# Splitting the two late norms of a two-block transformer layer between two output units, with weight halves placed between the tiles, and folding the end of the last product

## Chip, cores and metric

One NeuronCore of a Trainium2 chip runs the whole program. The metric is device time in microseconds (us); the median of several executions is compared.

## Reference

Two blocks run one after the other on x, a 256 x 2048 float32 matrix (sequence x width). The change touches the end of the second block only:

```python
        mix = (gate_a * ya + gate_b * yb) @ w_out[i]
        h = h + rmsnorm(mix, g_mix_post[i])
        u = rmsnorm(h, g_ffn_pre[i])
        up = causal_depthwise_conv_2(u @ w_up[i], conv_w[i], conv_b[i])
        gate_ff, value = jnp.split(up, [D_FF_2], axis=-1)
        f = (jax.nn.gelu(gate_ff, approximate=True) * value) @ w_down[i]
        h = h + rmsnorm(f, g_ffn_post[i])
        e = p[i] @ w_ple_in[i]
        h = h + jax.nn.sigmoid((h @ w_ple_gate[i]).astype(jnp.float32)).astype(h.dtype) * e
```

## The kernel before

Activations lie transposed: width on the 128 partitions (16 tiles of 128), the 256 positions along the free axis. Every product is made of **units**: a unit is 256 output columns over the whole inner dimension, and one unit is four **pieces** of four k tiles each (three pieces in ffn_down2). A piece's weights are one 512 KB transfer into `raw`. ScalarE casts them to their high half (`w_high`), VectorE subtracts to get the low half (`w_low`), and TensorE forms high x high, high x low and low x high, so the sum is nearly exact float32. Rings of four slots hold raw, high and low, so a piece's high half can be cast only when TensorE has finished the piece four before it.

A unit accumulates in one of two PSUM banks, `ps`, which alternate. Left half of a bank: products with x's high half; right half: high weights with x's low half. When the unit is done ScalarE copies the right half (`bcopy`), VectorE adds it (`summ`), and the unit's epilogue follows. In a **folded** unit both products go to the left half, in six matmuls of 256 columns for a k tile instead of two of 512 and two of 256; such a unit needs no copy and no add.

`Phase` objects list the products; `unit_no`, `piece_no`, `after` give the semaphore values. Each engine runs its own program in written order, and waits on semaphores for the others. `skewed` and `threaded` interleave the weight halves of later units with the epilogue of a unit.

The two **late norms** are the places where x has to be made new from the sum of squares of a whole product:

- **First late norm**, after `w_out2_end`: h + rmsnorm(mix), then the gain of the next norm; x goes into `act_a`, and `ffn_up0` (u @ w_up) reads it. The division by the second norm's rms is deferred to that product's epilogues (`rms(4)`, `recip(4)`, then `summ * rstd`). Its sum of squares is the matmul group `ssq_h`, which before stands after half of ffn_up0's second unit.
- **Second late norm**, after `ffn_down2_end`: h + rmsnorm(f); x goes into `act_a` for `ple_gate`.

In both, TensorE runs `gap`: the sum of squares, with the product p @ w_ple_in (8 groups of six matmuls, "ple") as filler around it. ScalarE takes the root (`rms`), VectorE the reciprocal (`recip`). `post_norm` then makes the tiles two at a time: VectorE scales (L1826), VectorE or GpSimd adds to the residual (L1831, L2048: pairs 0, 3, 6 on VectorE, the other five on GpSimd), ScalarE makes x's high half (L1356 or L1359), VectorE its low half (L1838 or L1843). The first unit of the next product takes the tiles as they come (`need_pn`), the weights of its four pieces having been prepared ahead of the norm.

The program ends with `ple_gate`, 8 units: sigmoid(h @ w) times e (in `gates`), added to h by GpSimd (L1963) and stored.

Of the kernel before, what the change touches and what calls it, by code (L numbers as in the profile page):

```python
# [21 lines left out]
ALU = mybir.AluOpType  # L22
# [100 lines left out]
def last_direct(ph, j):  # L123

    return ph.name in ("w_out2_end", "ffn_down2_end") and j == ph.U - 1


def plan():
# [23 lines left out]
    for g, n in enumerate((8, 8, 6)):  # L152
        ph.append(Phase("upconv", 2 * n, 2, 4, name=f"ffn_up{g}", group=g))
# [6 lines left out]
    ph.append(Phase("final", 8, 2, 4, name="ple_gate"))  # L160
# [58 lines left out]
def build(nc, A, out):  # L219
# [4 lines left out]
    with ExitStack() as ctx:  # L224
# [48 lines left out]
        def pcol(name, i=0):  # L273
# [67 lines left out]
        def source(ph, i, j, s):  # L341
# [26 lines left out]
            elif n.startswith("ffn_up"):  # L368
                w, c = "w_up_2", i * 256 + (j * DFF2 + ph.group * D)
# [6 lines left out]
            else:  # L376
                w, c = "w_ple_gate_2", u * 256
# [3 lines left out]
        def slot(ph, j, s):  # L381
            return (2 * s + j if ph.name == "proj_0" else j * ph.ppu + s) % RING
# [112 lines left out]
        def dst_tile(ph, i, j):  # L495
# [18 lines left out]
            if ph.kind == "upconv":  # L514
                return i * 2
# [12 lines left out]
        ADD_DVE, ADD_POOL = (0, 3, 6), (1, 2, 4, 5, 7)  # L528
# [42 lines left out]
        def _(sp):  # L571
# [24 lines left out]
            for ph in PH[1:]:  # L596
                def body(i, ph=ph):
                    for j in range(ph.U):
                        for s in range(ph.ppu):
                            n, at = piece_no(ph, i, j, s), slot(ph, j, s)  # L600
                            src = source(ph, i, j, s)
                            kn = src.shape[1]
                            sp.wait_ge(split_done, n + 1)
                            sp.dma_start(raw[:, at, 0:kn * S].rearrange("p (t n) -> p t n", t=kn),
                                         src).then_inc(raw_full[at], 16)
                over(sp, body, 0, ph.bodies)

            fin = BY["ple_gate"]
# [7 lines left out]
        def _(pe):  # L616
# [84 lines left out]
            for s in range(4):  # L701
                for j in range(2):
                    piece(p0, from_buf(act_a), None, 0, j, s, need_x)
# [35 lines left out]
            def gap(n, ph, ple_ph):  # L739
# [3 lines left out]
                take(fill, 1)  # L743
                ssq_last(ph)
                take(fill)

# [224 lines left out]
            gap(3, BY["w_out2_end"], BY["ple0"])  # L971
# [6 lines left out]
            def ssq_h():  # L978

                pe.wait_ge(pn_added, 2)  # L980
                pe.wait_ge(rms_ready, 4)
                parts = [sqacc[:, 0, :], sqacc[:, 1, :], G[:, 24, :], G[:, 25, :]]
                for c, part in enumerate(parts):
                    last = nc.tensor.matmul(pm[:, 3, 0:S], ones, part, start=(c == 0), stop=(c == 3))
# [8 lines left out]
            gap(5, BY["ffn_down2_end"], BY["ple1"])  # L993
            units(BY["ple_gate"], from_buf(act_a), None, lambda: None, need_pn(16))
# [3 lines left out]
        def _(act):  # L998
# [23 lines left out]
            def epilogue(ph, i, j):  # L1022
                k, g, n = ph.kind, bank(ph, j), unit_no(ph, i, j)
                t0 = dst_tile(ph, i, j)
                if last_direct(ph, j):
                    if k == "mix":
# [8 lines left out]
                act.wait_ge(w_used, end_piece(ph, i, j))  # L1035
                act.wait_ge(summed, n + 1)
                nc.scalar.copy(bcopy[:, g], ps[:, g, :, S:2 * S]).then_inc(b_copied, 1)  # L1037
# [32 lines left out]
            def stages(ph, i, j):  # L1070
# [14 lines left out]
                def base():  # L1085
# [4 lines left out]
                    c0 = i * 2 + (16 * ph.group + 44 * j)  # L1090
# [250 lines left out]
            def post_norm(n, ph, ple_ph, gain):  # L1341

                half = ple_ph.half
                rms(n)
# [3 lines left out]
                ple_out(ple_ph, 0)  # L1348
                for b in range(8):
                    if b in ADD_DVE:  # L1350
                        act.wait_ge(pn_r_dve, len(ADD_DVE) * half + ADD_DVE.index(b) + 1)
                    else:
                        act.wait_ge(pn_r_pool, len(ADD_POOL) * half + ADD_POOL.index(b) + 1)
                    if gain:
                        for k in (2 * b, 2 * b + 1):
                            nc.scalar.activation(act_a[:, k, 0:S], PJ[:, k, :], ACT.Copy,  # L1356
                                                 scale=pcol(gain, k)).then_inc(pn_high, 1)
                    else:
# [750 lines left out]
```

## Time and profile before

| | |
|---|---|
| median of 3 executions | 2986.57 us (2985.01 to 2989.87) |
| profiled execution: its own time | 2986.37 us |
| profiled execution: span | 2984.6 us |
| TensorE busy | 2939.8 us, 99% of the span |
| VectorE, ScalarE, GpSimd busy | 1915.2, 1533.6, 247.0 us |
| mean granted TensorE clock | 0.997 of full |

TensorE is busy nearly all the time, so the span is its work plus the few places where it waits. Times in the rows are microseconds from the span's start. The first late norm lies at about 2107 to 2145, the second at about 2863 to 2902, and the end is at 2977 to 2984.

### The profile page before, as it was taken

To read this page: it belongs to the slowest core of one execution; us is meant where nothing else is said; L and a number is where in the kernel's file an instruction comes from. 1 tells how busy PE (TensorE), PEld (TensorE's weight loads), DVE (VectorE), ACT (ScalarE), POOL (GpSimd) and SP (SyncE) were. 2 spreads that over 40 slices of the span, in tenths; PEclk is the share of its full clock that TensorE was granted. 3 is DMA by queue.
4 is the path that set the end of the run, shared out by engine and by line. 5 is a ranking of instruction groups with operands and counts; after the bars stand their busy time and mean duration, and the time that the engine had idled before them with its cause. 6 is when DMAs were issued, how large, how long until landed. Compare 5 with 4: busy or idle time off the path is not lost. (4 is left out here: it accounts for less than half of the span.)

```text
span 2984.6 us, 49193 instructions
## 1 busy us (share of the span) xinstructions
PE 2939.8 (99%) x17298; PEld 2583.4 (87%) x17298; DVE 1915.2 (64%) x2171; ACT 1533.6 (51%) x1909; POOL 247.0 (8%) x204
## 2 busy tenths in 40 slices
PE   8999999999999999999999999999999999999999
PEld 7888898988888888888888888988788888888877
DVE  6586665556665656656656666655777567657664
ACT  5576644444544444444544446445566455545554
POOL 3010020102101010000200000001200000010121
PEclk9999999999999999999999999999999999999999
DMA  8565557665566665665665545656466666566545
GB/s 241 162 175 159 169 179 218 190 172 188 189 190 190 190 190 183 197 188 180 197 190 178 169 149 166 197 169 199 147 196 184 190 189 190 185 188 190 169 150 161
DMA packets 543393, 544.85 MB, mean 183 GB/s; under 512 B 17096, under 2 KB 541896, under 8 KB 543280
## 3 DMA queue, kind: packets, MB, share of 16 engines
q1 hardware_dynamic: 541184, 537.32, 58.6%
q0 software_dynamic: 2096, 6.07, 0.7%
q8 instruction: 65, 1.06, 0.2%
q14 instruction: 48, 0.39, 0.0%
HBM read 541.23 MB, written 2.10 MB: 182 GB/s over the span
## 5 line engine op out<-in xcount | busy, mean ns | idle before, releaser
L1399 DVE TENSOR_TENSOR w_low<-raw,w_high 128x1024 fp32r<-128x1024 f32 x1016 | 1254.6, 1250 | 813.7 <-ACT w_high L1012 807.0
L1012 ACT CAST w_high<-raw 128x1024 fp32r<-128x1024 f32 x1016 | 1051.9, 1049 | 979.5 <-PE ps_gemm L649 945.0
L644 PE MATMUL ps_gemm<-act_a,w_high 128*128 128x512 f32 x4480 | 1449.0, 396 | 22.0 <-DVE act_a L1552 9.9
L644 PE MATMUL ps_gemm<-act_b,w_high 128*128 128x512 f32 x3208 | 1046.1, 396 | 6.9 <-DVE act_b L1408 4.6
L649 PEld LDWEIGHTS ps_gemm<-act_a,w_low 128*128 128x128 f32 x4608 | 865.2, 189 | 154.4
L649 PE MATMUL ps_gemm<-act_a,w_low 128*128 128x256 f32 x4608 | 993.7, 279 | 0.0
L644 PEld LDWEIGHTS ps_gemm<-act_a,w_high 128*128 128x128 f32 x4480 | 720.1, 189 | 69.5 <-issue 11.1
L649 PE MATMUL ps_gemm<-act_b,w_low 128*128 128x256 f32 x3520 | 780.0, 279 | 0.0
L649 PEld LDWEIGHTS ps_gemm<-act_b,w_low 128*128 128x128 f32 x3520 | 653.9, 189 | 97.3
L644 PEld LDWEIGHTS ps_gemm<-act_b,w_high 128*128 128x128 f32 x3208 | 524.9, 188 | 50.5 <-issue 4.9
L1441 DVE TENSOR_TENSOR summ<-ps_gemm,bcopy 128x512 f32<-128x512 f32 x227 | 155.4, 685 | 19.2 <-ACT bcopy L1037 19.1
L1037 ACT COPY bcopy<-ps_gemm 128x512 f32<-128x512 f32 x242 | 140.2, 579 | 22.5 <-PE ps_gemm L649 22.4
L1936 POOL TENSOR_TENSOR proj<-proj,summ 128x512 f32 x32 | 41.4, 1292 | 1008.0 <-DVE summ L1441 1008.0
L1510 DVE SCALAR_TENSOR_TENSOR gates<-summ,params,gates 128x254 f32<-128x254 f32 (+1 forms) x176 | 77.3, 481 | 18.6 <-ACT gates L1093 11.2
L1452 DVE TENSOR_TENSOR summ<-summ,rstd 128x512 f32<-128x512 f32 x124 | 85.9, 692 | 4.3
L1922 POOL TENSOR_TENSOR proj<-proj,summ 128x512 f32 x32 | 55.6, 1737 | 374.2 <-DVE summ L1496 374.2
L639 PE MATMUL ps_gemm<-act_b,w_high 128*128 128x256 f32 x312 | 82.6, 286 | 2.5 <-DVE proj L1491 2.3
L641 PE MATMUL ps_gemm<-act_b,w_high 128*128 128x256 f32 x312 | 82.3, 285 | 0.0
L1057 ACT CAST act_a<-summ 128x512 f32 (+1 forms) x32 | 19.9, 622 | 96.8 <-DVE summ L1465 96.8
L639 PEld LDWEIGHTS ps_gemm<-act_b,w_high 128*128 128x128 f32 x312 | 60.5, 194 | 2.9 <-issue 2.9
L1044 ACT ACTIVATE gates<-summ 128x512 f32<-128x512 f32 (+1 forms) x40 | 25.3, 632 | 69.5 <-DVE summ L1452 69.4
L641 PEld LDWEIGHTS ps_gemm<-act_b,w_high 128*128 128x128 f32 x312 | 60.6, 194 | 0.0
(285 smaller groups left out, 1227.1 us busy)
## 6 DMA issues: line engine op xcount, KB each, us to landing
raw<-in_w_in SPq DMA_DIRECT2D x352, 512.0 KB, 4.2
raw<-in_w_up SPq DMA_DIRECT2D x176, 512.0 KB, 3.5
raw<-in_w_mlp_up SPq DMA_DIRECT2D x128, 512.0 KB, 3.9
raw<-in_w_mlp_down SPq DMA_DIRECT2D x128, 512.0 KB, 3.5
raw<-in_w_down SPq DMA_DIRECT2D x88, 512.0 KB, 4.6
raw<-in_w_out SPq DMA_DIRECT2D x64, 512.0 KB, 4.7
raw<-in_w_branch SPq DMA_DIRECT2D x32, 512.0 KB, 4.3
raw<-in_w_ple_gate SPq DMA_DIRECT2D x32, 512.0 KB, 4.5
```

The source lines that it names most:

```text
L639: nc.tensor.matmul(ps[:, g, t, 0:S], wh[:, at, o:o + P], high(x), start=first, stop=False, skip_group_check=True)
L641: nc.tensor.matmul(ps[:, g, t, 0:S], wh[:, at, o:o + P], x[:, S:2 * S], start=False, stop=False, skip_group_check=True)
L644: nc.tensor.matmul(ps[:, g, t, :], wh[:, at, o:o + P], x, start=first, stop=False, skip_group_check=True)
L649: return nc.tensor.matmul(ps[:, g, t, 0:S], wl[:, at, o:o + P], high(x), start=False, stop=final, skip_group_check=True)
L1012: nc.scalar.copy(wh[:, at, :], raw[:, at, :]).then_inc(high_ready, 1)
L1037: nc.scalar.copy(bcopy[:, g], ps[:, g, :, S:2 * S]).then_inc(b_copied, 1)
L1399: nc.vector.tensor_tensor(wl[:, at, :], raw[:, at, :], wh[:, at, :].bitcast(F32), ALU.subtract).then_inc(split_done, 1)
L1441: nc.vector.tensor_tensor(s2, A_half, bcopy[:, g], ALU.add).then_inc(summed, 1)
L1452: nc.vector.tensor_tensor(s2, s2, r2, ALU.mult).then_inc(scaled, 1)
L1510: last = nc.vector.scalar_tensor_tensor(out=y[:, t, sh:S], in0=summ[:, g, t, 0:S - sh], scalar=pcol("conv_w2", c0 + t + 88 * tap), in1=y[: ...
L1922: nc.gpsimd.tensor_tensor(d, d, s2, ALU.add).then_inc(merged if split else epi_done, 1)
L1936: nc.gpsimd.tensor_tensor(d, d, s2, ALU.add).then_inc(epi_done, 1)
```

## The change

Around both late norms the next product's first two units form a phase of their own (`ffn_up0_0`, `ple_gate_0`). They are **woven**: TensorE runs piece s of unit 0 and then piece s of unit 1, so that a quarter of x (four tiles) is used by two units before the next quarter is needed. VectorE now makes every add, and GpSimd has none; the first four tiles go one at a time, the others in pairs. The casts and subtractions of the weight halves stand between the tiles. The sums of squares of the first norm are added by VectorE (`add_squares`), and `ssq_h` stands after the first unit of the remaining `ffn_up0`. Two units' epilogues then follow by hand. The table for the root is loaded ahead of the last square. At the second late norm ScalarE copies the third unit of ffn_down2_end and casts the first high half before it squares. The last two units of ple_gate are a phase `ple_gate_end`, whose second unit is folded: ScalarE takes the sigmoid straight from PSUM and VectorE makes the last add.

The core of the diff:

```diff
 def last_direct(ph, j):
-    return ph.name in ("w_out2_end", "ffn_down2_end") and j == ph.U - 1
+    return ph.name in ("w_out2_end", "ffn_down2_end", "ple_gate_end") and j == ph.U - 1
...
+def steps(ph):
+    if woven(ph):
+        return [(j, s) for s in range(ph.ppu) for j in range(ph.U)]
+    return [(j, s) for j in range(ph.U) for s in range(ph.ppu)]
...
 # TensorE
+            def two_units(ph, buf, need):
+                for j, s in steps(ph):
+                    piece(ph, from_buf(buf), None, 0, j, s, need if j == 0 else None)
...
-                    units(BY["ffn_up0"], from_buf(act_a), None, ssq_h, need_pn(0), (1, 1))
+                    two_units(BY["ffn_up0_0"], act_a, need_pn(0))
+                    units(BY["ffn_up0"], from_buf(act_a), None, ssq_h)
...
 # ScalarE, from the root on
                 rms(n)
+                ple_out(ple_ph, 0)
+                for k in range(4):
+                    high_x(k)
+                ple_out(ple_ph, 1)
                 gain_post(ph.kind, 14)
+                high_x(4, 2)
+                squares(0)
+                piece(then, 0, 0, 2)
+                high_x(6, 2)
+                high_x(8, 2)
+                squares(4)
+                high_x(10, 2)
+                piece(then, 0, 1, 2)
+                piece(then, 0, 0, 3)
...
 # ScalarE, after the first late norm
+            copy_half(w0, 0, 0)
+            piece(w1, 0, 0, 0)
+            copy_half(w0, 0, 1)
+            for s in range(1, 4):
+                piece(w1, 0, 0, s)
+            piece(w1, 0, 1, 0)
+            rms(4)
+            gate, value = stages(w0, 0, 0), stages(w0, 0, 1)
+            gate[1]()
+            piece(w1, 0, 1, 1)
+            value[1]()
+            gate[3]()
+            piece(w1, 0, 1, 2)
+            piece(w1, 0, 1, 3)
+            value[3]()
...
 # ScalarE, after the second late norm
+            epilogue(w0, 0, 0)
+            piece(w1, 0, 0, 0)
+            epilogue(w0, 0, 1)
+            for s in range(1, 4):
+                piece(w1, 0, 0, s)
...
 # VectorE
+            def add_norm(half, k, n=1):
+                dve.wait_ge(pn_gain, 8 * half + k // 2 + 1)
+                nc.vector.tensor_tensor(t, PJ[:, 16 + k:16 + k + n, :], r2, ALU.mult).then_inc(pn_t, n)
+                dve.wait_ge(pn_t, 16 * half + k + n)
+                nc.vector.tensor_tensor(d, d, t, ALU.add).then_inc(pn_r, n)
...
+                if k == "final" and last_direct(ph, j):
+                    dve.wait_ge(acted, after("acted", ph, i, j))
+                    nc.vector.tensor_tensor(s2, s2, tiles(G, t0, 2), ALU.mult).then_inc(scaled, 1)
+                    nc.vector.tensor_tensor(tiles(PJ, t0, 2), tiles(PJ, t0, 2), s2, ALU.add).then_inc(epi_done, 1)
```

Three places in the order of the built programs carry the prediction.

VectorE in the first late norm, before: from the reciprocal (gates is the scaled product, proj the residual, act_a is x).

```order
L1538 RECIPROCAL rstd<-rms 128x256 [waits rms_ready]
L1826 TENSOR_TENSOR gates<-proj,rstd 128x512 [waits pn_gain,rstd_ready]
L1831 TENSOR_TENSOR proj<-proj,gates 128x512 [waits pn_t]
L1826 TENSOR_TENSOR gates<-proj,rstd 128x512 [waits pn_gain] x3
L1838 SCALAR_TENSOR_TENSOR act_a<-proj,params,act_a 128x256 [waits pn_high]
L1838 SCALAR_TENSOR_TENSOR act_a<-proj,params,act_a 128x256
L1831 TENSOR_TENSOR proj<-proj,gates 128x512 [waits pn_t]
```

The changed program on VectorE, tiles 4 to 7 of the same norm and what follows them:

```order
L1938 TENSOR_TENSOR gates<-proj,rstd 128x512 [waits pn_gain]
L1940 TENSOR_TENSOR proj<-proj,gates 128x512 [waits pn_t]
L1947 SCALAR_TENSOR_TENSOR act_a<-proj,params,act_a 128x256 [waits pn_high]
L1947 SCALAR_TENSOR_TENSOR act_a<-proj,params,act_a 128x256
L1938 TENSOR_TENSOR gates<-proj,rstd 128x512 [waits pn_gain]
L1940 TENSOR_TENSOR proj<-proj,gates 128x512 [waits pn_t]
L1947 SCALAR_TENSOR_TENSOR act_a<-proj,params,act_a 128x256 [waits pn_high]
L1947 SCALAR_TENSOR_TENSOR act_a<-proj,params,act_a 128x256
L1484 TENSOR_TENSOR w_low<-raw,w_high 128x1024 [waits high_ready]
```

A pair's scale, add and low half now stand right behind each other, where three scales stood in a row before, and weight halves have moved in among the pairs.

ScalarE at the second root of the first late norm, before: the last square, the four high halves of the second unit, then the root.

```order
L1364 ACTIVATE gates<-proj 128x1024
L1012 CAST w_high<-raw 128x1024 [waits w_used,raw_full0]
L1012 CAST w_high<-raw 128x1024 [waits w_used,raw_full1]
L1012 CAST w_high<-raw 128x1024 [waits w_used,raw_full2]
L1012 CAST w_high<-raw 128x1024 [waits w_used,raw_full3]
L1126 ACTIVATE rms<-ps_small,stat 128x256 [waits rstd_ready,ssq_ready]
```

The same place in the changed program; the first cast is that of piece 0 of unit 1 of ffn_up0, the later three those of its pieces 1, 2 and 3.

```order
L1040 CAST w_high<-raw 128x1024 [waits w_used,raw_full0]
L1164 ACTIVATE rms<-ps_small,stat 128x256 [waits rstd_ready,ssq_ready]
L1131 ACTIVATE gates<-summ,params 128x256 [waits scaled,epi_done]
L1131 ACTIVATE gates<-summ,params 128x256
L1040 CAST w_high<-raw 128x1024 [waits w_used,raw_full1]
L1131 ACTIVATE gates<-summ,params 128x256 [waits scaled]
L1131 ACTIVATE gates<-summ,params 128x256
L1139 ACT_TABLE_LOAD [waits epi_done]
L1139 ACTIVATE gates<-gates 128x512 [waits acted]
L1040 CAST w_high<-raw 128x1024 [waits w_used,raw_full2]
L1040 CAST w_high<-raw 128x1024 [waits w_used,raw_full3]
```

Three of the unit's four high halves have moved from ahead of the root to behind it.

ScalarE after the second late norm in the changed program, from the last weight half of `ple_gate_0` on; the casts behind are pieces 0 and 1 of the next unit. Before, eight casts stood here ahead of the first copy.

```order
L1040 CAST w_high<-raw 128x1024 [waits w_used,raw_full3]
L1055 COPY bcopy<-ps_gemm 128x512 [waits summed,w_used]
L1106 ACT_TABLE_LOAD
L1106 ACTIVATE summ<-summ 128x512 [waits summed]
L1040 CAST w_high<-raw 128x1024 [waits w_used,raw_full0]
L1055 COPY bcopy<-ps_gemm 128x512 [waits summed,w_used]
L1106 ACTIVATE summ<-summ 128x512 [waits summed]
L1040 CAST w_high<-raw 128x1024 [waits w_used,raw_full1]
```

A unit's whole epilogue now stands ahead of the next unit's first weights.

## Rows read from the trace of the kernel before

**Rows 1.** The page, busy time, share of the span and instructions.

```profile
PE 2939.8 (99%) x17298; PEld 2583.4 (87%) x17298; DVE 1915.2 (64%) x2171; ACT 1533.6 (51%) x1909; POOL 247.0 (8%) x204
```

**Rows 2.** Waits of TensorE: in total, times, longest (us).

```profile
PE ps_small L715 <- ACT sqt L1111: 1.1, 1, 1.1
```

**Rows 3.** Stretches: length, busy PE, PEld, DVE, ACT, POOL, clock, DMA share, GB/s.

```profile
2095.77:2107.29 11.52, 11.52 (x98) 11.52 (x97) 5.44 (x5) 6.12 (x8) 1.29 (x1) 1.00 0.63 191
2114.91:2118.59 3.68, 0.01 (x2) 0.03 (x1) 3.68 (x4) 2.13 (x5) 3.25 (x2) 0.87 0.01 2
2118.59:2124.39 5.80, 5.77 (x17) 4.63 (x18) 5.80 (x8) 4.39 (x8) 3.77 (x3) 0.50 0.00 0
2124.39:2137.37 12.98, 9.88 (x49) 7.65 (x49) 12.95 (x18) 8.00 (x12) 4.88 (x4) 1.00 0.01 1
...
2804.79:2806.97 2.18, 0.40 (x4) 0.19 (x2) 1.36 (x2) 1.40 (x2) 0.00 (x0) 1.00 0.08 26
2806.97:2810.72 3.75, 3.75 (x12) 3.17 (x13) 3.50 (x3) 2.06 (x3) 0.00 (x0) 0.54 0.26 81
2880.81:2885.25 4.44, 0.00 (x1) 0.03 (x1) 4.44 (x5) 2.70 (x4) 3.31 (x2) 1.00 0.01 4
2885.25:2888.91 3.66, 3.66 (x13) 3.13 (x14) 3.66 (x5) 1.31 (x3) 1.90 (x2) 0.55 0.00 0
2888.91:2899.35 10.44, 9.88 (x53) 8.17 (x53) 9.09 (x11) 6.04 (x7) 3.10 (x2) 0.99 0.01 2
2902.19:2977.55 75.36, 75.35 (x433) 65.56 (x432) 39.40 (x38) 37.27 (x42) 12.37 (x7) 1.00 0.58 184
```

**Rows 4.** VectorE, groups by form: count, busy, mean ns of one, idle before.

```profile
L1399 DVE TENSOR_TENSOR w_low<-raw,w_high 128x1024 fp32r<-128x1024 f32 x1016 | 1254.6, 1250 | 813.7 <-ACT w_high L1012 807.0 <-DVEq L1494 3.1
...
L1452 DVE TENSOR_TENSOR summ<-summ,rstd 128x512 f32<-128x512 f32 x124 | 85.9, 692 | 4.3
...
L1510 DVE SCALAR_TENSOR_TENSOR gates<-summ,params,gates 128x255 f32<-128x255 f32 x88 | 38.7, 481 | 12.9 <-ACT gates L1093 11.2
...
L1826 DVE TENSOR_TENSOR gates<-proj,rstd 128x512 f32<-128x512 f32 x16 | 16.0, 1021 | 0.1
...
L1408 DVE TENSOR_TENSOR act_a<-proj,act_a 128x256 fp32r<-128x256 f32 x20 | 7.5, 419 | 2.6 <-ACT act_a L1299 1.5 <-ACT act_a L1259 1.1
```

**Rows 5.** ScalarE, groups by form, the same columns.

```profile
L1012 ACT CAST w_high<-raw 128x1024 fp32r<-128x1024 f32 x1016 | 1051.9, 1049 | 979.5 <-PE ps_gemm L649 945.0 <-DMA raw<-in_w_in 32.6 <-DMA raw<-in_w_out 0.3
...
L1093 ACT ACTIVATE gates<-summ,params 128x256 f32<-128x256 f32 x88 | 48.2, 596 | 23.2 <-DVE summ L1452 20.6 <-issue 0.4
...
L1356 ACT ACTIVATE act_a<-proj,params 128x256 fp32r<-128x256 f32 x16 | 7.1, 500 | 7.3 <-POOL proj L2048 4.7 <-DVE proj L1831 2.6
```

**Rows 6.** VectorE and ScalarE in order of time: start, length, instruction.

```profile
2110.95 1.75 DVE L1538 RECIPROCAL rstd<-rms 128x256 f32<-128x256 f32 x1 [0.52 <-ACT rms L1126]
...
2152.28 1.28 ACT L1101 ACT_TABLE_LOAD   x1
2153.57 0.63 ACT L1101 ACTIVATE gates<-gates 128x512 f32<-128x512 f32 x1
...
2875.55 1.28 ACT L1126 ACT_TABLE_LOAD   x1
2876.85 0.47 ACT L1126 ACTIVATE rms<-ps_small,stat 128x256 f32<-128x256 f32 x1
...
2877.35 1.75 DVE L1538 RECIPROCAL rstd<-rms 128x256 f32<-128x256 f32 x1 [0.56 <-ACT rms L1126]
```

**Rows 7.** The end, in order of time.

```profile
2977.58 0.59 ACT L1037 COPY bcopy<-ps_gemm 128x512 f32<-128x512 f32 x1 [7.52 <-PE ps_gemm L649]
2978.20 0.69 DVE L1441 TENSOR_TENSOR summ<-ps_gemm,bcopy 128x512 f32<-128x512 f32 x1 [7.41 <-ACT bcopy L1037]
2978.92 0.63 ACT L1068 ACTIVATE summ<-summ 128x512 f32<-128x512 f32 x1 [0.76 <-DVE summ L1441]
...
2980.70 1.26 POOL L1963 TENSOR_TENSOR proj<-proj,summ 128x512 f32 x1 [8.27 <-DVE summ L1472]
```

More of the change, by code:

```diff
@@ L700, in need_x @@
                     pe.wait_ge(lo0, 4 * s + k + 1)
-            for s in range(4):
-                for j in range(2):
-                    piece(p0, from_buf(act_a), None, 0, j, s, need_x)
+            for j, s in steps(p0):
+                piece(p0, from_buf(act_a), None, 0, j, s, need_x)
             def ssq_before(n, ph):
@@ L737, in ple, with gap @@
                         yield
-            def gap(n, ph, ple_ph):
+            def gap(n, ph, ple_ph, ahead):
                 fill = ple(ple_ph)
                 ssq_before(n, ph)
-                take(fill, 1)
+                take(fill, ahead)
                 ssq_last(ph)
                 take(fill)
+            def two_units(ph, buf, need):
+                for j, s in steps(ph):
+                    piece(ph, from_buf(buf), None, 0, j, s, need if j == 0 else None)
             pe.wait_ge(in_common, 16)
@@ L978, in ssq_h @@
             def ssq_h():
-                pe.wait_ge(pn_added, 2)
+                pe.wait_ge(pn_added, 1)
                 pe.wait_ge(rms_ready, 4)
-                parts = [sqacc[:, 0, :], sqacc[:, 1, :], G[:, 24, :], G[:, 25, :]]
-                for c, part in enumerate(parts):
-                    last = nc.tensor.matmul(pm[:, 3, 0:S], ones, part, start=(c == 0), stop=(c == 3))
+                for c in range(4):
+                    last = nc.tensor.matmul(pm[:, 3, 0:S], ones, G[:, 16 + c, :], start=(c == 0), stop=(c == 3))
                 last.then_inc(ssq_ready, 1)
@@ L1034, in epilogue @@
                     return
[L1035 to L1037 removed]
+                if not copied:
+                    copy_half(ph, i, j)
                 if k == "gate":
@@ L1347, in post_norm @@
                 gain_post(ph.kind, 14)
[L1348 to L1358, printed above, removed]
-                        nc.scalar.copy(act_a[:, 2 * b:2 * b + 2, 0:S], PJ[:, 2 * b:2 * b + 2, :]).then_inc(pn_high, 2)
-                    if b == 1:
-                        ple_out(ple_ph, 1)
-                    if gain and b % 2:
-                        t = 2 * b - 2
-                        nc.scalar.activation(G[:, 16 + t:20 + t, :], PJ[:, t:t + 4, :], ACT.Square).then_inc(pn_sq, 1)
-            def first_pieces(ph, pend):
-                for s in range(3):
-                    piece(ph, 0, 0, s)
-                pend()
-                piece(ph, 0, 0, 3)
+                high_x(4, 2)
[7 more added lines that the diff above has]
+                piece(then, 0, 0, 3)
+                high_x(12, 2)
+                squares(8)
+                high_x(14, 2)
+                piece(then, 0, 1, 3)
+                squares(12)
             pend = phases(["w_out2"], pend)
@@ new lines, in post_norm @@
+            def post_norm(n, half, gain, then, fourth):
+                recip(n)
+                add_norm(half, 0)
+                add_norm(half, 1)
+                low_x(half, gain, 0)
+                add_norm(half, 2)
+                low_x(half, gain, 1)
+                add_norm(half, 3)
+                low_x(half, gain, 2)
+                low_x(half, gain, 3)
+                if fourth:
+                    piece(then, 0, 1, 1)
+                add_norm(half, 4, 2)
+                low_x(half, gain, 4, 2)
+                add_norm(half, 6, 2)
+                low_x(half, gain, 6, 2)
+                piece(then, 0, 0, 2)
+                add_norm(half, 8, 2)
+                low_x(half, gain, 8, 2)
+                add_norm(half, 10, 2)
+                low_x(half, gain, 10, 2)
+                piece(then, 0, 1, 2)
+                piece(then, 0, 0, 3)
+                add_norm(half, 12, 2)
+                low_x(half, gain, 12, 2)
+                add_norm(half, 14, 2)
+                low_x(half, gain, 14, 2)
+                piece(then, 0, 1, 3)
@@ L1888, in _ @@
-            post_norm(5, 1, None)
-            dve.wait_ge(epi_done, BY["ple1"].unit0 + 2 + 2)
-            pend = skip_first(BY["ple_gate"])
-            pend()
+            down, w0, w1 = BY["ffn_down2_end"], BY["ple_gate_0"], BY["ple_gate"]
+            pieces(down, 0, 0)
+            pend()
+            for j in range(3):
+                pieces(down, 0, j + 1)
+                epilogue(down, 0, j)
+            piece(w0, 0, 0, 0)
+            piece(w0, 0, 1, 0)
+            epilogue(down, 0, 3)
@@ L2065, in _ @@
             run("ffn_down2_end")
-            for b in ADD_POOL:
-                add(b, 1)
+            run("ple_gate_0")
             run("ple_gate")
+            run("ple_gate_end")
 def kernel(**inputs):
```

273 lines of the change are left out of this document (166 added, 107 removed).

## Prediction

> **What bounds the kernel now.** I read the page first. TensorE is busy 99% of the span [rows 1], so only three things can move the time: TensorE's work, the places where it waits, and what follows its last matmul. The view of its waits and a table of stretches place the idle time at the two late norms; the timeline then gives the order in which each engine works there, the groups by form give durations.
>
> The unit of account is a piece (four k tiles). The undisturbed stretch before the end holds 432 matmuls, 27 pieces of 16, in 75.36 us: 2.79 us a piece, 11.17 a unit. A folded unit takes 11.52 [rows 3].
>
> At the first late norm the filler ends at 2114.91. The first unit then would end at 2126.1, yet unit 1 starts at 2137.37: TensorE stands 3.68 us, runs 5.80 us at a granted clock of 0.50 and is then fed slowly, and 11.3 us are lost. At the second the filler ends at 2880.81, unit 0 at 2899.35 instead of 2892.0: 7.4 us lost, with 4.44 us of standing and 3.66 us at 0.55 [rows 3]. A further 1.1 us are waited for the last square [rows 2]. These 20 us are what there is to win.
>
> **First norm, the tiles.** TensorE's need falls to four tiles in 5.58 us, since two units use each quarter. The question is how fast VectorE makes them. The 16 scales of before take 1.02 us each in the mean, where the same shape takes 0.69 elsewhere [rows 4]; beside them GpSimd was adding. With no GpSimd work there I use 0.69. A wait on an op just finished costs some 0.04 us (the end's chain goes from 2978.92 + 0.63 on in such steps, and 2977.58 + 0.59 to 2978.20) [rows 7]. A following independent op starts about 0.1 before the one ahead ends: 0.60 and 1.14 us of pitch for 0.69 and 1.25, an estimate from the timeline.
>
> In the new order scale, add, high half and low half of a pair are one chain: 0.73 + 0.73, then two 256-wide activations on ScalarE (0.50 each, second 0.39 later, so 0.93 with the wait) [rows 5], then two low halves of 0.48, 0.40 apart: 3.2 us a pair, in which VectorE stands idle while ScalarE casts. Two pairs and two weight halves of 1.14 [rows 4] make 8.7 us for a quarter, not 5.58. So VectorE sets the pace still.
>
> The start: the root's table load now lies ahead of the last square, so the reciprocal comes some 0.4 earlier than 2110.95 [rows 6] and ends at 2112.3. Four single tiles (0.42 an op [rows 4]) take 4.9, to 2117.2. Six pairs take 19.1, three weight halves between them 3.4, waits for their high halves 0.2, the last weight half 1.3: 2141.2. Woven unit 1's last piece ends at 2144.0. Before, unit 1 ended, ssq_h aside, at 2137.37 + 11.17 = 2148.5. **Won: 4.5 us.**
>
> **First norm, the handover.** Here I look at what stands behind the new waits. Ahead of ssq_h only piece 0 of ffn_up0's unit 1 has its halves; pieces 1, 2 and 3 have their casts behind the second root on ScalarE. After ssq_h TensorE has 2.79 us of work. Piece 1 needs: the sum's drain 0.36 (an estimate from the timeline), root 0.47, reciprocal 1.75 [rows 6], scale 0.69 [rows 4], base of the convolution 1.0 (two activations of 0.60, overlapping), cast 1.05 [rows 5], low half 1.25 [rows 4], six hand-overs 0.2: 6.8 us. TensorE stands 4.0 us. Then piece 2: four taps of 0.48 (1.9), scale 0.69 [rows 4], base 1.0, table load 1.28, gelu 0.6 [rows 6], cast 1.05, low half 1.25, less 0.1 of overlap: 7.6 us against 2.9: it stands 4.7. Before, all four pieces were ready here. The first two pieces of ffn_up0 cost 0.3 (low halves behind sums), and each restart 0.1. **Lost: 9.2 us.** The norm together: +4.7 us. The DMAs are not late: piece n's transfer starts when piece n-4 is split, and the stretches in question ran at up to 0.01 of the DMA engines [rows 3].
>
> **Second norm.** Third unit's copy and the first cast are ahead, so the last add doesn't wait behind three weight halves, the 1.1 us of [rows 2] go and the table load (2875.55) is off the path: reciprocal at 2875.6 instead of 2877.35 [rows 6], end 2877.4. No gain here, so high and low half are one op of 0.62 and 0.69: 2.7 us a pair. Four single tiles 4.7, six pairs 16.3, four weight halves 4.6 with waits, the last one 1.3, some 0.4 of waiting for it: 2904.7; unit 1's last piece ends at 2907.5. Before, unit 1 ended at 2899.35 + 11.17 = 2910.5. Won: 3.0. The handover: from the end of unit 0, copy 0.6 [rows 7], sigmoid's table 1.28, sigmoid 0.6, cast 1.05, low half 1.25 make 4.7 against 2.79 (with drain): 2.1 us stall; then product, sum, sigmoid, cast, low half, 4.1 against 2.9: 1.2 us; restarts 0.2. Lost: 3.5. The folded unit adds 11.52 - 11.17 = 0.35. **Together: +0.85 us.**
>
> **The end.** Before: copy, sum, sigmoid, product, then GpSimd to 2981.96 from 2977.58 [rows 7], 4.38 us. Now sigmoid 0.63, product 0.69, add 0.69 with waits 0.07: 2.1. **-2.3 us.** The last transfer is as before.
>
> **TensorE's clock.** A tile takes 0.70 us at 2.4 GHz. After standing for 3.68, 4.44 and most of 2.18 us it ran 5.80, 3.66 and 3.75 us at 0.50 to 0.55, the 1.2 GHz level [rows 3]; 12 or 13 matmuls in 3.7 us instead of 2.1 is 1.6 us lost a time. The change takes away the first two and puts in stalls of 4.0, 4.7 and 2.1 us and several of 1 to 1.8. Inside a norm, or just ahead of another stall, the slow clock costs nothing, since VectorE is awaited; behind the 4.7 and the 2.1 it is exposed, in part. Nothing here shows how much: between 0 and three such stretches (4.8 us) I take one and a half, 2.5 us.
>
> The Trainium skill's page "TensorE: Matmul & The Clock Gate" (HAM oscillation — how this bites in real kernels) says that idle gaps between bursts bring the throttle back, each next burst starting cold, which speaks against an order that trades one long gap for several. By that rule each stall of handover length would pay, and the sum would take the upper bound, +2.3 us; the rows with 0.50 to 0.55 agree for gaps from 2.2 us up.
>
> **The sum**: +4.7 + 0.85 - 2.3 + 2.5 = +5.75 us on the profiled execution's 2986.37: 2992.1. The median of the runs lies 0.2 above that execution, so 2992.2 us, +0.19%.
>
> **Rivals.**
> - *The clock stays full* behind the new stalls. For it: the stalls are split, and waits of 1.1 to 1.3 us brought no slow stretch. Against: 2.18 us did [rows 3]. 2992.2 - 2.5 = 2989.7.
> - *The clock falls at each, or hops cost more.* Three exposed stretches add 2.3; if a hop costs 0.1 instead of 0.04, the 36 hops of the twelve pairs add 2.2, about half of them on the path with the rest of the chain: together 2996.
> - *The handover costs half*, because VectorE and ScalarE get ahead of the order I assumed. Only the written order speaks, and it is against it. 2992.2 - 4.4 - 1.0 (less slow clock) = 2986.8, no change at all.
> - *The other side: VectorE keeps pace.* If a pair took 2.2 us or less, a quarter would cost TensorE's 5.58 and no tile would be awaited: unit 1 would end at 2114.9 + 22.3 = 2137.2 and, with the filler 1.1 earlier, at 2879.7 + 22.3 = 2902.0: 6.8 and 5.5 us sooner, with some slow clock gone: 2979. For it: the slowed scales show how much GpSimd's adds took [rows 4]. Against: the chain's own durations.
> - *A drain at each table load.* The table load costs its 1.28 us again at each switch. In the trace the gelu starts at 2153.57, 0.01 after the load's end [rows 6], so it costs 1.28 and no more. If another 1.4 us went with each of the two loads that are newly on the path, the time would be 2995. The Trainium skill's page "ScalarE: Activation LUTs" (What ACT_TABLE_LOAD costs) puts the whole switch at 2.66 us, 1.38 of them a drain; the trace does not agree.
>
> **How the numbers follow.** What a measurement can tell from no change is about 0.2%, 6.0 us. The forecast has 0.56, its own range 2990.0 to 2994.5, half on each side of 2992.5; full clock 0.13; clock or hops 0.14; half the handover 0.09; pace kept 0.05; drain 0.03. Faster 0.05. Within: 0.28 + 0.13 + 0.09 = 0.50. Slower: 0.28 + 0.14 + 0.03 = 0.45. The range takes in full clock and reaches into the half handover below and the clock's case above: 2987 to 2996.5.
>
> **What the changed profile would show.** TensorE's waits for x (now L664 on L1947, L1951) come in several pieces of 0.2 to 1.8 us in either norm, where single ones of 3.68 and 4.44 stood; none over 2 us. No GpSimd add, and scales of 0.69 us. Two stalls of some 4.0 and 4.7 us on `w_low` within 12 us, 50 us after the first norm's start, and two of 2.1 and 1.2 us behind ple_gate_0. The end: sigmoid, product, add, 2.1 us to the last transfer. Wrong would be: no stall on `w_low` after ssq_h, pairs made in 2.2 us, or a slow stretch in each of the gaps.

## The result and the profile after

| | before | after |
|---|---|---|
| median | 2986.57 us (2983.44 to 2989.87, 9 runs) | 2993.51 us (2992.84 to 3000.91, 9 runs) |
| ratio after / before | | 1.0028, 95% interval 1.0019 to 1.0037 |
| profiled execution, span | 2984.6 us | 2993.5 us |

The change makes the kernel slower. The medians differ by 6.9 us (0.23%); the ratio of 1.0028 is worked out over all runs, and one of after's, 3000.91, stands far from the rest. The forecast was 2992.2 (+0.19%). The profiled execution of after took 2995.9 us, 2.4 above its median, so I first ask where its span differs. TensorE has a few waits that both programs share, and they serve as marks. Rows of TensorE's timeline, before:

```profile
2023.21 0.73 PE L644 MATMUL ps_gemm<-act_b,w_high 128*128 128x512 f32 x2 [1.33 <-DVE act_b L1408]
2316.26 0.73 PE L644 MATMUL ps_gemm<-act_b,w_high 128*128 128x512 f32 x2 [0.73 <-DVE act_b L1408]
2837.99 0.70 PE L644 MATMUL ps_gemm<-act_b,w_high 128*128 128x512 f32 x2 [1.32 <-DVE w_low L1399]
```

The same three matmuls after:

```profile
2025.99 0.72 PE L664 MATMUL ps_gemm<-act_b,w_high 128*128 128x512 f32 x2 [1.33 <-DVE act_b L1493]
2325.26 0.72 PE L664 MATMUL ps_gemm<-act_b,w_high 128*128 128x512 f32 x2 [0.73 <-DVE act_b L1493]
2846.97 0.70 PE L664 MATMUL ps_gemm<-act_b,w_high 128*128 128x512 f32 x2 [1.31 <-DVE w_low L1484]
```

Ahead of the first mark the work is the same, and 2.78 us of the 8.9 arise there: they are no part of the change. One piece of it is the stretch at 232.60 below, where the clock fell to 0.53 while TensorE was busy all the time, just behind some 3 us of small matmuls (8 or 64 partitions). At this place of the program the clock fell in the profiled executions of after, e1, e3, e5 and e8, and stayed at 1.00 in those of before, e2, e4, e6, e7 and e9: it comes and goes from one execution to the next, and the distances between the marks leave it out.

From the first mark to the second, around the first late norm, the distance grows from 293.05 to 299.27: **+6.22 us**. From the second to the third nothing happens (521.73 and 521.71). From the third to the end of the span, over the second norm and the program's end, 146.61 becomes 146.53: **-0.08 us**. Inside the span the change costs 6.1 us. A further 0.5 lies outside it: the time less the span is 1.75 to 1.88 us in all runs of before and 2.29 to 2.40 in those of after. No run here was made for that half microsecond, and its cause is open; e4, e8 and e9 below stand at 1.8 to 1.9, the other changed kernels at 2.2 to 2.4.

TensorE's waits after, from 2100 to 2990 (total, times, longest), against the single waits of 3.68 and 4.44 us in [rows 3]:

```profile
PE ps_gemm L664 <- DVE w_low L1484: 11.1, 5, 3.7
PE ps_gemm L664 <- DVE act_a L1947: 5.3, 5, 1.5
PE ps_gemm L664 <- DVE act_a L1951: 5.1, 7, 1.2
...
```

The waits for x (L1947, L1951) are short, as intended. The row that has grown is `w_low`: the weights' low halves are late five times (before, three waits of 2.3 us in all stood here). The fifth is the third mark. The other four stand at the two handovers, the places where the woven pair's epilogues and the next unit's weight halves fall together. In TensorE's timeline:

```profile
2167.43 0.73 PE L664 MATMUL ps_gemm<-act_a,w_high 128*128 128x512 f32 x2 [3.72 <-DVE w_low L1484]
2175.08 1.22 PE L664 MATMUL ps_gemm<-act_a,w_high 128*128 128x512 f32 x2 [3.05 <-DVE w_low L1484]
2920.11 0.72 PE L664 MATMUL ps_gemm<-act_a,w_high 128*128 128x512 f32 x2 [2.01 <-DVE w_low L1484]
2924.18 0.72 PE L664 MATMUL ps_gemm<-act_a,w_high 128*128 128x512 f32 x2 [1.02 <-DVE w_low L1484]
```

The table of stretches around them (length, busy PE, PEld, DVE, ACT, POOL, clock, DMA share, GB/s):

```profile
232.60:236.20 3.60, 3.60 (x12) 2.64 (x12) 3.50 (x9) 1.91 (x2) 0.00 (x0) 0.53 0.87 294
2163.72:2167.43 3.71, 0.00 (x0) 0.00 (x1) 1.51 (x3) 2.02 (x3) 0.00 (x0) 1.00 0.75 263
2167.43:2172.03 4.60, 4.60 (x16) 3.79 (x16) 3.28 (x8) 2.21 (x3) 0.00 (x0) 0.63 0.37 114
2172.03:2175.08 3.05, 0.00 (x1) 0.00 (x0) 1.97 (x4) 2.67 (x4) 0.00 (x0) 0.98 0.00 0
2175.08:2178.70 3.62, 3.62 (x12) 3.09 (x13) 3.58 (x6) 2.05 (x3) 0.00 (x0) 0.55 0.53 158
2178.70:2182.30 3.60, 3.60 (x23) 3.16 (x23) 3.02 (x6) 3.08 (x5) 0.00 (x0) 1.00 0.71 218
2920.11:2923.16 3.05, 3.05 (x16) 2.50 (x16) 1.41 (x3) 1.86 (x3) 1.30 (x1) 1.00 0.52 167
```

Behind each of the two long stalls TensorE runs a piece wholly or mostly at the 1.2 GHz level: 16 matmuls in 4.60 us (0.63 in the mean) instead of 2.79, then 12 in 3.62 (0.55) instead of 2.09. The first excess (1.81) lies ahead of another wait for VectorE; the second (1.53) is paid. Behind the stall of 2.01 us the clock stayed at 1.00.

ScalarE tells why piece 1 is late:

```profile
2160.96 0.48 ACT L1164 ACTIVATE rms<-ps_small,stat 128x256 f32<-128x256 f32 x1 [7.07 <-PE ps_small L1009]
2164.09 1.09 ACT L1131 ACTIVATE gates<-summ,params 128x256 f32<-128x256 f32 x2 [2.65 <-DVE summ L1507]
2165.09 1.03 ACT L1040 CAST w_high<-raw 128x1024 fp32r<-128x1024 f32 x1
2169.80 1.09 ACT L1131 ACTIVATE gates<-summ,params 128x256 f32<-128x256 f32 x2 [3.68 <-DVE summ L1507]
2170.91 1.28 ACT L1139 ACT_TABLE_LOAD   x1
2172.20 0.63 ACT L1139 ACTIVATE gates<-gates 128x512 f32<-128x512 f32 x1
2172.74 1.97 ACT L1040 CAST w_high<-raw 128x1024 fp32r<-128x1024 f32 x2
```

It stands idle for 7.07, 2.65 and 3.68 us with casts queued behind the waiting instruction. VectorE's pairs, first norm and second:

```profile
2120.03 0.68 DVE L1938 TENSOR_TENSOR gates<-proj,rstd 128x512 f32<-128x512 f32 x1
2120.82 0.69 DVE L1940 TENSOR_TENSOR proj<-proj,gates 128x512 f32<-128x512 f32 x1
2122.49 0.88 DVE L1947 SCALAR_TENSOR_TENSOR act_a<-proj,params,act_a 128x256 fp32r<-128x256 f32 x2 [0.98 <-ACT act_a L1387]
2123.29 0.68 DVE L1938 TENSOR_TENSOR gates<-proj,rstd 128x512 f32<-128x512 f32 x1
...
2893.20 0.69 DVE L1940 TENSOR_TENSOR proj<-proj,gates 128x512 f32<-128x512 f32 x1
2894.71 0.69 DVE L1951 TENSOR_TENSOR act_a<-proj,act_a 128x512 fp32r<-128x512 f32 x1 [0.81 <-ACT act_a L1390]
2895.32 0.69 DVE L1938 TENSOR_TENSOR gates<-proj,rstd 128x512 f32<-128x512 f32 x1
2896.11 0.69 DVE L1940 TENSOR_TENSOR proj<-proj,gates 128x512 f32<-128x512 f32 x1
```

A pair takes 3.26 us (2120.03 to 2123.29) and 2.91 us (2893.20 to 2896.11), 0.98 and 0.81 of it waiting for ScalarE. The scale is down to 0.68 from the 1.02 of [rows 4]. The end, against [rows 7]:

```profile
2988.94 0.60 ACT L1064 ACTIVATE summ<-ps_gemm 128x512 f32<-128x512 f32 x1 [7.89 <-PE ps_gemm L669]
2989.57 0.69 DVE L1523 TENSOR_TENSOR summ<-summ,gates 128x512 f32<-128x512 f32 x1 [7.79 <-ACT summ L1064]
2990.30 0.69 DVE L1526 TENSOR_TENSOR proj<-proj,summ 128x512 f32<-128x512 f32 x1
```

From its first instruction to the end of the span it takes 4.6 us; before it took 7.0 (2977.58 to 2984.6).

### The profile page after: what moved, and what is told of

The parts are those of the page before. It is cut to its first block and busy times, and to the rows that moved or that the text cites. A ratio compares the mean times of both kernels' runs of the same rounds, so it can differ in the third digit from the quotient of the medians.

```text
span 2993.5 us, 49048 instructions
## 1 busy us (share of the span) xinstructions
PE 2944.0 (98%) x17330; PEld 2587.1 (86%) x17330; DVE 1913.6 (64%) x2192; ACT 1510.6 (50%) x1892; POOL 228.3 (8%) x191
```

## The experiments

My theory: the tiles come a little sooner, but behind both norms the written order puts the next unit's weight halves behind instructions that wait, and that costs more than the tiles give. The rival: the loss is made in the norms (the chain of a pair) or by the clock, and the stalls on `w_low` only use up slack. All edits are on the changed kernel. The last columns are the distances between the marks in the one profiled execution of each kernel, which are free of what happens elsewhere. They repeat well where an edit doesn't touch a place: 299.26 and 299.29 (e3, e4) against 299.27, and 146.42 to 146.47 (e1, e2, e8, e9) against 146.53. The medians are less sharp: of the 12 runs of e5 the fastest took 2976.39 us at a mean clock of 1.000 and the slowest 2985.88 at 0.997.

| kernel | median us | ratio to before, 95% | mark 1 to 2 | mark 3 to end |
|---|---|---|---|---|
| before | 2986.6 | | 293.05 | 146.61 |
| after | 2993.51 | 1.0028 (1.0019 to 1.0037) | 299.27 | 146.53 |
| e1_halves_ahead | 2988.85 | 1.0009 (1.0000 to 1.0017) | 295.50 | 146.42 |
| e2_early_ssq | 2983.85 | 0.9998 (0.9989 to 1.0007) | 288.98 | 146.44 |
| e3_gate_halves_ahead | 2991.11 | 1.0015 (1.0006 to 1.0024) | 299.26 | 143.16 |
| e4_end_as_before | 2996.20 | 1.0036 (1.0023 to 1.0049) | 299.29 | 148.65 |
| e5_both_handovers | 2981.02 | 0.9976 (0.9968 to 0.9985) | 288.98 | 143.18 |
| e6_next_pair_first | 2983.30 | 0.9992 (0.9983 to 1.0000) | 294.35 | 141.89 |
| e7_all_three | 2969.28 | 0.9940 (0.9927 to 0.9953) | 283.31 | 138.38 |
| e8_gpsimd_beside | 2999.20 | 1.0044 (1.0030 to 1.0057) | 304.62 | 146.43 |
| e9_gpsimd_at_scales | 2998.86 | 1.0040 (1.0026 to 1.0053) | 305.15 | 146.47 |

**e1_halves_ahead.** On ScalarE, and the same on VectorE around `recip(4)`:

```diff
-            piece(w1, 0, 1, 0)
+            for s in range(4):
+                piece(w1, 0, 1, s)
             rms(4)
             gate, value = stages(w0, 0, 0), stages(w0, 0, 1)
             gate[1]()
-            piece(w1, 0, 1, 1)
             value[1]()
             gate[3]()
-            piece(w1, 0, 1, 2)
-            piece(w1, 0, 1, 3)
             value[3]()
```

> Edit: behind the first late norm the high and low halves of pieces 1, 2 and 3 of ffn_up0's second unit are made ahead of the second root and reciprocal; ssq_h stays where it is. Theory (the loss sits in the order behind the norm): TensorE's stalls of 3.72 and 3.05 us on w_low at 2167 and 2175 vanish with their 3.2 us of half clock, 9.9 us in all; but the epilogues of ffn_up0_0 now run with no weight halves among them, the sum of ffn_up0's first unit comes 12.5 us after ssq_h's end and the halves of its third unit behind it, so TensorE waits 2.8 and 2.0 us there. Net -5 us: 2988.5. Rival (the tile chain inside the norm or the clock makes the loss, the stalls only use up slack): 2993.5, unchanged.

Measured: 2988.85, 4.7 below after (3.8 by the marks). Both stalls are gone. In their place one stall of 3.50 us, again at half clock, stands at the third unit:

```profile
2171.52 0.68 DVE L1552 TENSOR_TENSOR summ<-ps_gemm,bcopy 128x512 f32<-128x512 f32 x1
2172.24 0.69 DVE L1563 TENSOR_TENSOR summ<-summ,rstd 128x512 f32<-128x512 f32 x1
2172.85 1.22 DVE L1482 TENSOR_TENSOR w_low<-raw,w_high 128x1024 fp32r<-128x1024 f32 x1
```

The weight half ends at 2174.07, and TensorE starts at 2174.12. I had expected two waits of 2.8 and 2.0; it is one. The mechanism is the one named: moving halves alone gives 3.8 us and moves the rest of the stall to behind the epilogues, which ssq_h starts late. That ssq_h is what makes them late is shown by e2.

**e2_early_ssq.** TensorE's sum of squares two pieces sooner, and (second part) the order on VectorE for it:

```diff
-                    units(BY["ffn_up0"], from_buf(act_a), None, ssq_h)
+                    units(BY["ffn_up0"], from_buf(act_a), None, ssq_h, None, (0, 1))
...
             piece(w1, 0, 0, 0)
-            piece(w1, 0, 0, 1)
             add_squares((16, 20), (pn_sq, 2), sq_pair)
-            sum_halves(w0, 0, 1)
-            piece(w1, 0, 0, 2)
+            piece(w1, 0, 0, 1)
             add_squares((24, 28), (pn_sq, 4), sq_pair)
-            piece(w1, 0, 0, 3)
             add_squares((16, 24), (sq_pair, 2), pn_added)
-            piece(w1, 0, 1, 0)
+            piece(w1, 0, 0, 2)
+            sum_halves(w0, 0, 1)
+            piece(w1, 0, 0, 3)
             recip(4)
...
             scale_sum(w0, 0, 0)
-            piece(w1, 0, 1, 1)
+            piece(w1, 0, 1, 0)
             gate[1]()
             scale_sum(w0, 0, 1)
+            piece(w1, 0, 1, 1)
             value[1]()
```

ScalarE casts in the same order: all four pieces of the first unit ahead of the root, none of the second, and then one half of the second unit between two steps of the epilogues.

> Edit: ssq_h stands two pieces into the first unit of the remaining ffn_up0 instead of behind it, VectorE adds the squares ahead of the weight halves of those pieces, and behind the second root each engine makes one weight half between two steps of the epilogues. Theory: the whole handover cost goes, nothing new stands: -9.5 us with its slow clock, 2984.0. If the epilogues, not the place of ssq_h, were what is late, a stall of 2 to 5 us stays at the third unit: 2987 to 2989. Rival (tile chain or clock makes the loss): 2993.5.

Measured: 2983.85, and no wait on `w_low` from 2100 to 2200. By the marks the first norm is 10.29 us shorter than after, and 4.07 shorter than before. So the handover cost 10.3 us and the tiles had won 4.1. The rival is out: the stalls were no slack, and with them gone the norm is shorter than before. The 10.3 is made of the two stalls (3.72 and 3.05), the two pieces drawn out by the clock (1.81 and 1.53) and 0.2 that I don't place. What in the change wins the 4.1 (the weave, the adds taken from GpSimd, the single tiles) no run takes apart.

**e3_gate_halves_ahead.** On ScalarE (VectorE likewise):

```diff
-            epilogue(w0, 0, 0)
             piece(w1, 0, 0, 0)
+            piece(w1, 0, 0, 1)
+            epilogue(w0, 0, 0)
+            piece(w1, 0, 0, 2)
             epilogue(w0, 0, 1)
-            for s in range(1, 4):
-                piece(w1, 0, 0, s)
+            piece(w1, 0, 0, 3)
```

> Edit: behind the second late norm the high and low halves of pieces 0 and 1 of ple_gate's next unit stand ahead of the copy, table load and sigmoid of ple_gate_0. Theory: the stalls of 2.01 and 1.02 us on w_low at 2920 and 2924 go, -3.0 us: 2990.5. Rival (they hide behind another wait, that of the sum for the PSUM bank): at most 1 us less, 2992.5 to 2993.5.

Measured: 2991.11, 2.4 less between medians, 3.37 less by the marks. Both stalls behind ple_gate_0 are gone.

**e4_end_as_before.** `last_direct` without the new phase, so the last unit isn't folded:

```diff
-    return ph.name in ("w_out2_end", "ffn_down2_end", "ple_gate_end") and j == ph.U - 1
+    return ph.name in ("w_out2_end", "ffn_down2_end") and j == ph.U - 1
```

> Edit: the last unit of ple_gate_end is not folded; copy, sum, sigmoid, product and GpSimd's add follow it as before the change. Theory: the folded end is worth 2.45 us behind the last matmul (4.6 against 7.05 us) less 0.35 us of matmuls: +2.1 us, 2995.6. Rival (the end hides behind the transfer of the unit before): unchanged.

Measured: 2996.20, +2.7 between medians (five runs) and +2.12 by the marks. The folded end is a real gain inside the span. In time it is some 1.6, since without it 0.5 less lies outside the span (1.8 against 2.3); whether the fold is what costs that 0.5 is open, since e8 and e9 have the fold and stand at 1.8 too.

**e5_both_handovers.** The edits of e2 and e3 together.

> Edit: the earlier ssq_h with its order (as e2_early_ssq) and the gate halves ahead (as e3_gate_halves_ahead) together. Theory (two separate places, each on the path): the gains add, -9.7 and -2.4 us by the medians measured, 12 us from 2993.5: 2981.5, below the kernel before the change. Rival (they share a slack, or the clock gives part back): 2983.5.

Measured: 2981.02. The distances are those of e2 (288.98) and of e3 (143.18): the two places are independent, and the kernel is now 0.24% faster than before the change.

**e6_next_pair_first.** In `post_norm` on VectorE, for both norms:

```diff
+                add_norm(half, 4, 2)
                 if fourth:
                     piece(then, 0, 1, 1)
-                add_norm(half, 4, 2)
+                add_norm(half, 6, 2)
                 low_x(half, gain, 4, 2)
-                add_norm(half, 6, 2)
+                add_norm(half, 8, 2)
                 low_x(half, gain, 6, 2)
                 piece(then, 0, 0, 2)
-                add_norm(half, 8, 2)
+                add_norm(half, 10, 2)
                 low_x(half, gain, 8, 2)
```

and so on to the last pair.

> Edit on the changed kernel: in both norms VectorE scales and adds the next pair before it makes the low half of the last one, so it no longer waits 0.8 to 1.0 us a pair for ScalarE; the handovers stay as they are. Theory (the chain scale, add, high half, low half of 3.26 and 2.90 us a pair is the pace; VectorE's own work is some 2.2 and 2.0 us): nearly all of the 5.3 and 5.1 us that TensorE waits for x go, -9 us: 2984.5, and the stalls of 3.7, 3.1, 2.0 and 1.0 us on w_low stay where they are. Rival (the weight halves between the pairs set the pace, or the last pair's low half comes as late as before): at most 3 us less, 2990.5.

Measured: 2983.30, 10.2 less; 4.92 and 4.64 by the marks. TensorE's waits from 2085 on:

```profile
PE ps_gemm L664 <- DVE w_low L1484: 11.5, 6, 3.7
...
PE ps_gemm L664 <- DVE act_a L1951: 1.4, 4, 0.7
PE ps_gemm L664 <- DVE act_a L1947: 0.6, 2, 0.4
```

The waits for x fall from 10.4 to 2.0 us, and those on `w_low` stay (11.5 in all, against 11.1). Two stages of the norm on VectorE now stand as:

```profile
2124.53 0.69 DVE L1938 TENSOR_TENSOR gates<-proj,rstd 128x512 f32<-128x512 f32 x1
2125.32 0.69 DVE L1940 TENSOR_TENSOR proj<-proj,gates 128x512 f32<-128x512 f32 x1
2125.93 0.88 DVE L1947 SCALAR_TENSOR_TENSOR act_a<-proj,params,act_a 128x256 fp32r<-128x256 f32 x2
2126.72 0.68 DVE L1938 TENSOR_TENSOR gates<-proj,rstd 128x512 f32<-128x512 f32 x1
```

2.19 us a pair (2124.53 to 2126.72) with no wait for ScalarE: the "other side" rival of the prediction, made true by an order. It was priced at 6.8 and 5.5 us sooner, and gives 4.9 and 4.6, with 2.0 us of waits left.

**e7_all_three.**

> Edit: both handovers as in e5_both_handovers and the next pair ahead as in e6_next_pair_first. Theory: the gains add, 12 and 9 us: 2972.5. Rival (with the norm faster the sums of squares or the halves of the next unit are late in their turn): 3 to 5 us of stall on w_low or ps_small behind the norm, 2976 to 2978.

Measured: 2969.28, 0.6% below the kernel before and 24.2 us below after, 3.2 better than expected. Between marks 1 and 2 the two gains (10.29 and 4.92) would give 284.06; it is 283.31. No new wait came: from 2085 on TensorE waits 1.5 us on `w_low` (1.3 of them the third mark) and 2.0 for x.

**e8_gpsimd_beside.**

```diff
             run("w_out2_end")
+            for m in range(12):
+                pool.wait_ge(pn_t, 4 + 2 * (m // 2))
+                link(nc.gpsimd.tensor_tensor(sqacc[:], sqacc[:], sqacc[:], ALU.add))
             reset(4)
```

> Edit on the changed kernel: GpSimd makes 12 adds of 128x512 on its own scratch (which it clears afterwards) beside VectorE's pairs in the first late norm; nothing waits for them and the output is the same. Theory (GpSimd's adds were what made the scales of the kernel before 1.02 us instead of 0.69): scales and adds of the six pairs rise to about 1.0 us, the chain of a pair from 3.26 to some 3.9, and the time by 3 to 4 us: 2997. Rival (the 1.02 had another cause, such as reading PSUM or ScalarE's work beside them): 0.69 stays, 2993.5.

Measured: 2999.20, 5.7 more. VectorE by form, 2110 to 2160:

```profile
L1947 DVE SCALAR_TENSOR_TENSOR act_a<-proj,params,act_a 128x256 fp32r<-128x256 f32 x16 | 12.9, 838 | 5.9 <-ACT act_a L1387 5.9
...
L1940 DVE TENSOR_TENSOR proj<-proj,gates 128x512 f32<-128x512 f32 x6 | 4.2, 692 | 0.6
L1938 DVE TENSOR_TENSOR gates<-proj,rstd 128x512 f32<-128x512 f32 x6 | 4.1, 678 | 0.0
```

The time rose more than the 3 to 4 us expected, and my expectation named the wrong instructions: scales and adds stayed, the low halves went from 482 to 838 ns.

**e9_gpsimd_at_scales.** The same with `pn_low` in place of `pn_t`.

> Edit: the same 12 adds of GpSimd on its scratch as in e8_gpsimd_beside, but two of them start as each low half of a pair ends, so they run beside VectorE's scale and add of the next pair and not beside its low halves. In e8 the low halves rose from 0.48 to 0.84 us while scales and adds stayed at 0.68 and 0.69. Theory (one VectorE instruction is drawn out for each GpSimd add, whichever is next to start behind the add's own start): now scales or adds rise, by 0.5 to 1 us a pair each, low halves stay near 0.48 or less drawn out; the chain and the time as in e8, 2997 to 3000. Rival (a scalar_tensor_tensor of 256 columns is the only form that is slowed): scales and adds stay at 0.69 and the time at 2993.5.

Measured: 2998.86. The same view:

```profile
L1940 DVE TENSOR_TENSOR proj<-proj,gates 128x512 f32<-128x512 f32 x6 | 7.4, 1234 | 0.6
L1947 DVE SCALAR_TENSOR_TENSOR act_a<-proj,params,act_a 128x256 fp32r<-128x256 f32 x16 | 7.2, 481 | 6.0 <-ACT act_a L1387 6.0
...
L1938 DVE TENSOR_TENSOR gates<-proj,rstd 128x512 f32<-128x512 f32 x6 | 5.8, 965 | 0.0
```

Now scales and adds are drawn out (965 and 1234 ns) and the low halves are not (481). One weight half is drawn out too (two of them took 3.21 us in place of 2.36). So it isn't the form: it is whatever VectorE would start while a GpSimd add is under way. The trace of before shows that the 1.02 us of [rows 4] are a mean of two kinds:

```profile
2886.39 1.66 POOL L2048 TENSOR_TENSOR proj<-proj,gates 128x512 f32<-128x512 f32 x1 [1.83 <-DVE gates L1826]
2886.83 1.76 DVE L1826 TENSOR_TENSOR gates<-proj,rstd 128x512 f32<-128x512 f32 x1
...
2892.02 0.68 DVE L1826 TENSOR_TENSOR gates<-proj,rstd 128x512 f32<-128x512 f32 x1
```

Of its ten scales that stand by themselves, the three that began with GpSimd in the middle of an add took 1.76, 1.77 and 1.77 us and the other seven 0.68 or 0.69.

## Why the prediction was right, step by step

Times of after are given less the offset at the nearest mark (2.78 in the first norm, 8.98 in the second).

- **First norm, the tiles.** Reciprocal's end: 2112.3 predicted, 2112.18 measured. Pair: 3.2 against 3.26. Last weight half: 2141.2 against 2141.7. Won: 4.5 against 4.1 (e2). Right. That VectorE's chain is the pace was shown by e6.
- **First handover.** Two stalls of 4.0 and 4.7 us were predicted, in this place and this order. The first is 3.72. The second is 3.05 of waiting behind a piece drawn out by 1.81, 4.86 together: the slow clock filled part of the wait for VectorE. Lost: 9.2 predicted; 10.29 by e2, less the 1.53 of exposed slow clock 8.8. Right. The 0.3 on the first two pieces did not come: TensorE has no wait on `w_low` between the norm and 2163.72.
- **Second norm, the tiles.** Reciprocal's end: 2877.4 predicted, 2877.5 measured. Unit 1's end: 2907.5 predicted; the stall at 2920.11 began at 2918.10, less 8.98 is 2909.1. Won: 3.0 predicted, 2910.5 - 2909.1 = 1.4 measured. **This term was mis-sized by 1.6 us**: a pair takes 2.91 us, not 2.7, which is 1.2 us in six pairs; the other 0.4 I did not place. Of a pair's 0.2 some 0.06 lie between scale and add (2895.32 to 2896.11 is 0.79, I had 0.73), the rest in the hand-overs to ScalarE and back (0.81 from the add's end to the low half, and ScalarE's part was 0.62).
- **Second handover.** Stalls of 2.1 and 1.2 us predicted, 2.01 and 1.02 measured; 3.5 with restarts, 3.37 by e3. Right.
- **The end.** -2.3 predicted, -2.46 measured (7.02 to 4.56), less 0.35 for the folded unit is 2.1; e4 gives 2.12.
- **The clock.** One and a half exposed slow stretches (2.5 us) predicted, as a guess between none and three; one was exposed (1.53 us), behind the stall of 3.05, and none behind 2.01. The prediction took [rows 3] to show a slow stretch behind a gap of 2.18 us; of these 0.40 are matmuls, and the wait itself is 1.78 us.

The sum: -4.1 + 8.8 + 1.5 - 1.4 + 3.4 + 0.35 - 2.5 = +6.05 against 6.14 by the marks and 5.75 in the prediction. Two errors, +1.6 (second norm) and -1.0 (clock), partly cancel, so the sum is closer than its terms are: that much is luck. The medians differ by 6.9, of which 0.5 lie outside the span.

Of the rivals, "the clock stays full" held behind one of the two handovers. "The handover costs half" fell with e2 (10.3 us) and e3 (3.4). "The other side" needed pairs in 2.2 us and got them only by the order of e6. "Hops cost more" came true in part, in the 1.2 us of the second norm; in the first a pair took 3.26 us against 3.2. "A drain at each table load" fell: after the two loads the next operation starts at 2172.20 and 2917.23, 0.01 us behind their ends. The Trainium skill's page "TensorE: Matmul & The Clock Gate" (HAM oscillation — how this bites in real kernels) tells of a kernel in which the wait between two bursts of matmuls brings the throttle back, so that each next burst starts cold. The traces agree for all waits of 3.0 us and more and not for those of 2.01 to 2.04 us (last section), so the upper bound of +2.3 us on the sum, which the prediction tied to that rule, was not reached.

## What to carry to other kernels

Behind a place where one engine must wait (a root, a table load, a reciprocal), look at what its written order has queued behind the waiting instruction, and count how many microseconds of work the bound engine still has in hand: here 2.8 us of matmuls stood against a chain of some 6.5 (2.79 and the stall of 3.72). Moving work ahead of such a wait gives only a part if what starts the chain is itself late (e1: 3.8 of 10.3 us); starting it sooner gave all of it back (e2). Where a chain over two engines leaves an idle stretch in each pair, try the order alone: with the next pair's first steps ahead of the last step of the one before, the waits for x fell from 10.4 to 2.0 us (e6). Read a small difference between two kernels by distances between marks that both share: 2.78 of the 8.9 us between these two spans had nothing to do with the change.

## What the runs showed of the hardware

**A slow stretch behind a stall costs some 1.56 us, and a stall of some 2 us need not bring one.** Ahead of the second norm all traces have a wait of 1.77 or 1.78 us for act_b. In the profiled executions of the eleven kernels it was followed by a clock of 0.53 to 0.65 in eight and of 1.00 in three (e6, e8, e9). The stretches behind it in after and in e6:

```profile
2815.95:2819.55 3.60, 3.60 (x13) 3.11 (x14) 3.39 (x3) 2.07 (x3) 0.00 (x0) 0.60 0.27 75
...
2808.46:2812.06 3.60, 3.60 (x21) 3.15 (x22) 3.40 (x3) 2.58 (x4) 0.00 (x0) 1.00 0.27 68
```

The first row is after, the second e6. Between marks 2 and 3 it makes 521.71 against 520.15, 1.56 us, where the prediction had estimated 1.6; the other nine traces have 521.70 to 521.73 or 520.13 to 520.17. Over the traces: in the 3.6 us behind stalls of 1.52 and 1.53 us the clock was always 1.00, as behind 1.84 and 1.89 us (e8); behind 2.01 to 2.04 us (ple_gate_0) always 1.00, in seven executions; behind 2.16 to 2.19 us (e8, e9) it was 0.53, 0.57, 0.69, 0.72 and 1.00; behind a wait of some 2.27 us between 665 and 673, which all eleven have, 0.59 to 0.72; behind 2.37 us (e8) 0.70; and behind 3.03 us and more, from 2100 on, always 0.50 to 0.60. The length of the stall alone doesn't decide, and what does is open; no run here was made for it.

**GpSimd and VectorE.** An add of 128x512 in SBUF on GpSimd holds up the instruction that VectorE would start beside it: in e9 by 0.65 us for most adds of a pair and 0.84 for two scales, in e8 by 0.36 us for each low half in the mean; GpSimd's own add takes 1.51 us in e9 against 1.28 in e8. VectorE's add at 2118.99 in e9 ends at 2120.33: GpSimd's first add began at 2118.37 and, with 1.28 us, ended at about 2119.65, and 0.69 more is 2120.34. The Trainium skill's page "SBUF — State Buffer" (SBUF: two separate sides) says that the two share a port pair as an exclusive lock, which whichever starts first keeps for its whole instruction, a VectorE operation with two SBUF inputs among those concerned. The traces agree: a wait to the other's end, not a slower rate. In before too, the add of 2886.39 ends at 2888.05, and the scale drawn out beside it at 2888.59, 0.54 later (a scale alone takes 0.68). Twelve such adds that nobody waited for cost the kernel 5.7 and 5.4 us between medians (5.35 and 5.88 by marks 1 to 2).
